# The causal mask of a decay attention, moved from matmul products into the decay rows

## What is computed

```python
c = jnp.cumsum(jax.nn.log_sigmoid(f_logit.astype(jnp.float32)), axis=1)   # per head, per token
s = jnp.einsum('bhtd,bshd->bhts', qi, k) * scale
s = s + ci[..., :, None] - c[:, :, None, :]
s = jnp.where(kpos[None, :] <= qpos[:, None], s, -jnp.inf)
p = jax.nn.softmax(s, axis=-1)
out = jnp.einsum('bhts,bshd->bthd', p, v)
```

## Time and profile before

| | |
|---|---|
| median of 3 runs | 934.23 us (931.28 to 938.12) |
| the profiled execution's own time | 933.19 us |
| its span | 931.5 us |
| TensorE busy | 912.9 us, 98% of the span |
| VectorE busy | 547.2 us, 59% |
| ScalarE busy | 301.2 us, 32% |
| the mixer's list, first scores to last | about 81 to 170 us |
| the chain that ended last | TensorE 89%, VectorE 4%, ScalarE 3% |

### The profile page before, as it was taken

One profiled execution on the slowest core, in us unless ns is written; L12 is line 12 of the kernel. 1 busy time (PEld: TensorE's weight loads), 2 busy tenths in 40 slices (PEclk: granted clock), 3 DMA queues, 4 the chain that ended last, 5 costly groups with the idle time before them and its releaser, 6 DMA issues.

```text
span 931.5 us, 13473 instructions
## 1 busy us (share of the span) xinstructions
PE 912.9 (98%) x4611; PEld 743.0 (80%) x4611; DVE 547.2 (59%) x936; ACT 301.2 (32%) x610; POOL 72.7 (8%) x138
## 2 busy tenths in 40 slices
PE   8999999999999999999999999999999999899998
PEld 7887776788888888888888888888878897568877
DVE  7257547265877677777634344686765363774554
ACT  7144466424222222222201112533321313453610
POOL 0000000010110010010001000000000000000000
PEclk9999999999999999999999999999999999999999
DMA  8756523254666556656655665476445212222554
GB/s 279 237 181 223 160 94 114 91 180 156 208 196 204 183 190 196 200 181 196 203 187 182 194 199 193 146 247 206 159 147 160 91 57 80 66 71 91 164 186 148
DMA packets 50214, 154.78 MB, mean 166 GB/s; under 512 B 9564, under 2 KB 10860, under 8 KB 50040
## 3 DMA queue, kind: packets, MB, share of 16 engines
q1 hardware_dynamic: 22320, 75.70, 25.6%
q0 software_dynamic: 19008, 69.21, 22.6%
q10 hardware_dynamic: 8840, 9.23, 3.1%
HBM read 149.63 MB, written 4.49 MB: 165 GB/s over the span
## 4 chain that ended last, share of the span: by engine, by line
PE 89%; DVE 4%; ACT 3%; issue 2%; DMA 2%; DVEq 0%; SPq 0%; POOLq 0%; ACTq 0%
PE bank L645 75%; PE bank L702 2%; DMA HI<-wstream 1%; PE bank L1054 1%; PE bank L1074 1%; PE bank L780 1%; PE bank L804 1%; PE bank L977 1%; PE bank L989 1%; PE bank L794 1%; DVE LO L1593 1%; PE bank L1004 1%; PE bank L1065 1%; DMA RAW<-wstream 0%; PE bank L783 0%
## 5 line engine op out<-in xcount | busy, mean ns | idle before, releaser
L645 PE MATMUL bank<-GH,HI 128*128 128x512 f32 (+1 forms) x724 | 292.4, 404 | 2.1 <-ACT DV L1435 1.4
L645 PE MATMUL bank<-GH,LO 128*128 128x512 f32 (+1 forms) x724 | 282.0, 390 | 0.0
L645 PE MATMUL bank<-GL,HI 128*128 128x512 f32 (+1 forms) x724 | 281.5, 389 | 0.0
L1593 DVE TENSOR_TENSOR LO<-RAW,HI 128x1024 fp32r<-128x1024 f32 x88 | 107.7, 1224 | 127.9 <-DMA HI<-wstream 127.0
L645 PEld LDWEIGHTS bank<-GH,HI 128*128 128x128 f32 x724 | 136.4, 188 | 34.9 <-issue 7.5
L645 PEld LDWEIGHTS bank<-GH,LO 128*128 128x128 f32 x724 | 136.1, 188 | 28.8
L645 PEld LDWEIGHTS bank<-GL,HI 128*128 128x128 f32 x724 | 136.6, 189 | 23.8
L627 POOL DMA_DIRECT2D HI<-wstream x132 | 70.2, 532 | 834.6 <-PE bank L645 824.7
L1309 ACT ACTIVATE YC<-AB,PAR 128x512 f32<-128x512 f32 x44 | 36.0, 819 | 140.7 <-DVE AB L1740 140.7
L645 PE MATMUL bank<-AH,HI 128*128 128x512 f32 x176 | 69.3, 394 | 0.0
L645 PE MATMUL bank<-AH,LO 128*128 128x512 f32 x176 | 69.0, 392 | 0.0
(11 more groups left out here) (304 smaller groups left out, 1209.4 us busy)
## 6 DMA issues: line engine op xcount, KB each, us to landing
RAW<-wstream SPq DMA_DIRECT2D x135, 512.0 KB, 3.7
HI<-wstream POOLq DMA_DIRECT2D x132, 512.0 KB, 4.9
X<-x_t SPq DMA_DIRECT2D x8, 256.0 KB, 7.6
NCB<-out_t ACTq DMA_DIRECT2D x4, 512.0 KB, 3.7
out_t<-X ACTq DMA_DIRECT2D x8, 256.0 KB, 5.8
XR<-out_t ACTq DMA_DIRECT2D x8, 256.0 KB, 3.6
out_t<-XR SPq DMA_DIRECT2D x7, 256.0 KB, 3.2
EG<-out_t ACTq DMA_DIRECT2D x1, 1024.0 KB, 5.1
```

Of the source, the lines that this page charges most:

```text
L645: mm = pe.matmul(out, a, b, start=(first and n == 0), stop=(last and n == 2))
L1593: dve.tensor_tensor(LO[:, u % RING, :], RAW[:, u % RING, :], HI[:, u % RING, :].bitcast(F32), ALU.subtract).then_inc(unit_split, 1)
```

## The change

The mask products, IDF, CSF and their two activations go. NCB keeps its size but is now two buffers (pairs by turns) of eight 128-element blocks for each of two heads. The DMAs of a pair (two, one per head) write the row's four blocks to places 1, 3, 5 and 7, in pieces of 512 bytes. VectorE then makes the other places in a new item `bias` p: a copy of block 0 to place 0 (2x128 elements per partition), masked copies of the blocks 0, 1, 2 at places 2, 4, 6 (2x3x128 elements, minus CAUSAL's diagonal block) and block 3 masked in place (2x128). `biased_max` reads 1 to 4 of these places with a constant stride: (2), (0, 4), (0, 3, 6) or (1, 3, 5, 7). From the third pair on, ScalarE's queue waits until the buffer's old maxima are made.

```diff
+        if n % 4 == 3 and n < 12:
+            slot.append(("bias", n // 4 + 1))
...
-    return (... + first[13:] + [("lowqk", 3)]
+    return (... + first[13:] + [("lowqk", 3), ("bias", 0)]
...
-        NCB = place("NCB", [P, 8, T], F32, arena + 80 * KB)
+        NCB = place("NCB", [P, 2, 2, 8, P], F32, arena + 80 * KB)
...
-                    pe.wait_ge(idr_made, 2)
...
-                        pe.matmul(PS[2 + e][:, 0:w], q[r, 4 + p, P * i:P * (i + 1)], k[r, p, 0:w],
-                                  start=(part == 0), stop=False)
-                for e in range(2):
-                    pe.matmul(PS[2 + e][:, P * i:w], IDF[:, :], CSF[:, :], start=False, stop=True).then_inc(s_made, 1)
+                        mm = pe.matmul(PS[2 + e][:, 0:w], q[r, 4 + p, P * i:P * (i + 1)], k[r, p, 0:w],
+                                       start=(part == 0), stop=(part == 2))
+                        if part == 2:
+                            mm.then_inc(s_made, 1)
...
-                    act.dma_start(NCB[:, 2 * n:2 * n + 2, :],
-                                  out_t[2 * n:2 * n + 2, :].unsqueeze(0).to_broadcast([P, 2, T]))\
-                       .then_inc(scratch_landed, 16)
+                    elif n >= 2:
+                        act.wait_ge(max_made, 8 * (n - 1))
+                    for e in range(2):
+                        head = out_t[2 * n + e, :].rearrange("(j c) -> j c", c=P)
+                        act.dma_start(NCB[:, n % 2, e, 1:8:2, :], head.unsqueeze(0).to_broadcast([P, NB, P]))\
+                           .then_inc(scratch_landed, 16)
...
-                dve.wait_ge(scratch_landed, 16 * (n // 4 + 1))
+                S = S.rearrange("p (j c) -> p j c", c=P)
+                bias = NCB[:, n // 4 % 2, e, (slice(2, 3), slice(0, 5, 4), slice(0, 7, 3), slice(1, 8, 2))[n % 4], :]
+                dve.wait_ge(biased, 3 * (n // 4 + 1))
...
+            def mask_bias(p):
+
+                rows = NCB[:, p % 2, :, :, :]
+                dve.wait_ge(scratch_landed, 32 * (p + 1))
+                dve.tensor_copy(rows[:, :, 0, :], rows[:, :, 1, :]).then_inc(biased, 1)
+                diagonal = CAUSAL[:, 384:512].unsqueeze(1)
+                dve.tensor_tensor(rows[:, :, 2:7:2, :], rows[:, :, 1:6:2, :],
+                                  diagonal.unsqueeze(1).to_broadcast([P, 2, 3, P]), ALU.subtract).then_inc(biased, 1)
+                dve.tensor_tensor(rows[:, :, 7, :], rows[:, :, 7, :], diagonal.to_broadcast([P, 2, P]), ALU.subtract)\
+                   .then_inc(biased, 1)
```

More of the change, by code:

```diff
@@ L61 @@
 STORED_NCB, STORED_ROWS, STORED_BETA, STORED_NT, STORED_XS = (16 * n for n in (1, 2, 3, 11, 12))
-LANDED_ROWS, LANDED_BETA, LANDED_MS, LANDED_XI = (16 * n for n in (5, 6, 7, 15))
+LANDED_ROWS, LANDED_BETA, LANDED_MS, LANDED_XI = (16 * n for n in (9, 10, 11, 19))
 _at = 0
@@ L222, in _mix1 @@
     first, last = products(0, 4), products(10, 12)
-    return (first[:3] + norms[:2] + first[3:4] + [("ncb", 0)] + _merge(first[4:13], norms[2:]) + first[13:] + [("lowqk", 3)]
+    return (first[:3] + norms[:2] + first[3:4] + [("ncb", 0)] + _merge(first[4:13], norms[2:]) + first[13:] + [("lowqk", 3), ("bias", 0)]
             + part(0, 4, products(4, 7)) + part(4, 8, _merge(products(7, 10), scaled))
@@ L379, in build @@
         SGB = place("SGB", [P, 4, P], F32, arena + 112 * KB)
-        IDF = place("IDF", [P, P], F32R, arena + 114 * KB)
-        CSF = place("CSF", [P, P], F32R, arena + 114 * KB + 512)
         assert arena + 115 * KB <= 229368, arena
@@ L506, in build @@
         sgw_masked = sem("sgw_masked")
-        idr_made, scratch_stored, scratch_landed = sem("idr_made"), sem("scratch_stored"), sem("scratch_landed")
+        biased, scratch_stored, scratch_landed = sem("biased"), sem("scratch_stored"), sem("scratch_landed")
         xs_made = sem("xs_made")
@@ L1239, in _ @@
             act.dma_start(out_t[0:8, :], FR[0:8, 2, :]).then_inc(scratch_stored, 16)
-            act.activation(IDF[:, :], IDENT, ACT.Copy).then_inc(idr_made, 1)
-            act.wait_ge(masks_landed, 16)
-            act.activation(CSF[:, :], CAUSAL[:, 384:512], ACT.Copy, scale=-1.0).then_inc(idr_made, 1)
             for what, n in MIX1_ORDER:
@@ L1652, in biased_max @@
                 S = PS[2 + e][:, 0:w]
-                dve.wait_ge(scratch_landed, 16 * (n // 4 + 1))
+                S = S.rearrange("p (j c) -> p j c", c=P)
+                bias = NCB[:, n // 4 % 2, e, (slice(2, 3), slice(0, 5, 4), slice(0, 7, 3), slice(1, 8, 2))[n % 4], :]
+                dve.wait_ge(biased, 3 * (n // 4 + 1))
                 dve.wait_ge(s_made, 2 * n + e + 1)
-                dve.tensor_tensor_reduce(S, S, NCB[:, 2 * (n // 4) + e, 0:w], -1.0, 3e38, ALU.add, ALU.min,
+                dve.tensor_tensor_reduce(S, S, bias, -1.0, 3e38, ALU.add, ALU.min,
                                          MX1[:, c:c + 1]).then_inc(max_made, 1)
+            def mask_bias(p):
[7 more added lines that the diff above has]
+                   .then_inc(biased, 1)
             for what, n in MIX1_ORDER:
@@ L1677, in _ @@
                     dve.tensor_tensor(rest, full, top.bitcast(F32), ALU.subtract).then_inc(qk_split, 1)
+                elif what == "bias":
+                    mask_bias(n)
                 elif what == "A":
```

## The result

The changed kernel takes 940.12 us (median of 20 runs, 938.17 to 944.82); the kernel before 934.14 us in 20 runs beside it. The ratio is 1.0069 with a 95% interval of 1.0056 to 1.0082: 6 us slower where 1.8 were forecast, and just past the upper end of the range (940.0). It is within 1%, so "no change by over 1%" held, but the range did not. The profiled execution took 940.21 us with a span of 938.5; that of before 933.19 and 931.5.

A forecast was written before the change was run, and what follows sets the result against it. TensorE bounds the kernel; masks about -3.0, bias0 and its stall +1.8, moved quarter +1.4, bias3, B9's wait and A11's new place +1.6 net +1.8 us: 936.0 us, range 930.5 to 940.

The forecast's parts named there:

- What bounds the kernel: TensorE, 98% busy at full clock throughout; removed work gains only where it ends last; shift at 191 us passes through.
- What the mask products cost: At the 16 mask pairs behind the scores: 0.28 us a pair by starts, 4.5 us in all.
- rival 2: Removal gives less than a pair's distance, as the following product pays the handover: 937.5 to 938.6 us; chance 0.12.
- What is added on VectorE: Each of four bias items takes 1.55 us (1.4 to 1.8); strided maxima add 0 to 0.1 us per item.
- bias0 and the first quarters: Before A1: bias0 delays A0's exponentials, A1 starts at 85.85, TensorE is +2.7 us behind after A1.
- moved quarter: One projection quarter fewer before A1, to be done afterwards: +1.4 us.
- A2 to A9: Six masks give -1.7 us, bias1 and bias2 are covered, A8's mask gives nothing; shift at A9 +1.0.
- A9 to A12: bias3 lies in full on the path before A12, which comes +1.9 to +2.4 us late; masks 11 to 14 give nothing.
- The end: A15's mask, in a full stretch, gives -0.28 us; net of the whole change +1.8 us.
- 1 (all hides): All bias items hide on VectorE: 928.3 to 929.7 us, or 932 if one partly hides; chance together 0.22.
- 3 (late rows): Row loads in 512-byte pieces take over 12 us and stall VectorE, then TensorE: 944 us or more; chance 0.03.
- 4: No work leaves TensorE's path, for instance if the new order opens an unseen wait over 2 us: 938 to 941; chance 0.06.

The follow-up runs named there:

- gap_filled: Changed kernel with 12 idle 512-column products on TensorE before A1's scores and 10 before A12's; 936.70 us, ratio 1.0034.
- early_kept: Changed kernel with the projections' quarters in their old places, bias0 behind lowqk2, last row load behind A8, bias3 behind A9; 933.86 us, ratio 1.0001.
- masks_out: Kernel before without the mask products and nothing in their place (no causal mask within the diagonal blocks); 934.16 us, ratio 0.9998.
- fills_kept: Changed kernel with the projections' quarters in the places of the kernel before, bias items put in afterwards; 937.51 us, ratio 1.0040.
- bias0_early: Changed kernel with bias0 alone moved ahead, behind lowqk2; 938.65 us, ratio 1.0054.
- order_only: Kernel before with the changed kernel's list order, bias items counted but empty, mask products kept; 935.64 us, ratio 1.0025.
- best_filled: early_kept with 3 idle products before A9's scores, 6 before A12's and 3 before A13's; 932.96 us, ratio 0.9986.

## Why the prediction was wrong, by its steps

- **What bounds the kernel**: held. TensorE is last but for the places named, and a shift at 191 us goes through to 583 us (+4.0 becomes +4.4). That the clock is full throughout was a misreading: the page's nines round away a slow stretch of 3.4 us that the kernel before has too, from 799.6 us. TensorE in order of time there:

```profile
798.30 0.52 PE L1065 MATMUL bank<-CON,P 128*128 128x128 f32 x3 [1.70 <-ACT PT L1507]
...
801.09 0.63 PE L645 MATMUL bank<-GL,HI 128*128 128x512 f32 x1
801.52 0.63 PE L645 MATMUL bank<-GH,LO 128*128 128x512 f32 x1
```

  An idle 1.70 us stands before it, so that a wait can bring the clock down could have been read before the change was run.
- **What the mask products cost**: mis-sized. 0.28 us a pair by the starts became 0.20. The products start where the mask did, as forecast, but the first one behind the scores now has 0.34 us to its successor (87.38 to 87.72 above), where behind a mask pair it had 0.28 (85.47 to 85.75), so a part of the handover stays. That is rival 2's mechanism in part, and over nine counted pairs it is +0.7 us. The formula in the Trainium skill ("VectorE: DVE Perf Modes", section on the trn2 errata) gave an estimate of 0.11 a pair. The measurement lies between the two, 0.09 above that and 0.08 below mine.
- **What is added on VectorE**: held (1.52 against 1.55), and so did the copy's and the maxima's prices.
- **bias0 and the first quarters**: the wait held to 0.1 us (A1 at 85.85 forecast, 86.49 - 0.65 = 85.84 measured). The step failed in what comes behind it: "TensorE is behind by +2.7 us after A1". I took TensorE's pace after a wait as its pace before it, since the page shows the clock full throughout. In the mixer's list it was full in a kernel whose longest wait there is 1.2 us. **The missing term is the clock: put at nothing, it cost 1.6 us between A1 and A2 in the profile, and filling both waits gives back 3.3 us of the timed runs (gap_filled)**; it is what carries the result out of the range. The sign that I gave, A1 to A8 shorter by 1.7 us, didn't come (45.84 us against 44.26), and it forgot my own moved quarter, which is done there: by my terms it should have read 0.3 shorter.
- **A2 to A9**: held, masks aside; bias1 and bias2 are covered, A8's mask gives nothing.
- **A9 to A12**: held (forecast +1.9 to +2.4 at A12; measured +4.2, of which 1.8 are the slow stretch behind A1). B9 waited 0.15 us.
- **The end**: A15's mask held with 0.2. The sum of the stalls, 1.8, stands against the 3.2 that gap_filled has left: 0.7 for the masks, 0.2 for the idle products' own length, some 0.3 for the second block in its profile.
- **Rivals**: 1 (all hides) was wrong. Even early_kept, where the items do hide, has 2.4 us of distance and not 4.5. 3 (late rows) was wrong: 6.3 us at the most. 4 named the right size for the wrong reason: no wait of over 2 us opened that I hadn't counted. None named the clock.

## What to carry to other kernels

A wait on a product engine that was always busy has two prices: its own length, and the clock behind it. Where a page shows the full clock, look with narrower windows for short slow stretches that it rounds away, and at the longest wait behind which the clock held; treat a longer one as unpriced. Work taken off TensorE in a sparse stretch lengthens the waits there, so a part of the gain can be lost to the clock (0.7 of 2.4 us in masks_out's profile); a few products whose results nobody reads may give it back. And an item that is only counted in a spread list is an edit of its own: here the moved quarters cost 1.7 us with nothing else changed.

## What the hardware did that I hadn't expected

- In the changed kernel's profile the granted clock fell to 1.2 GHz for 3.4 us, starting 1.9 us after TensorE had begun to work again behind an idle 2.88 us; not at once. In fills_kept it began 0.7 us after the start, and behind A12 it lasted 6.8 us there and in masks_out.
- The length of the wait alone doesn't tell whether it falls. In the mixer, behind an idle 1.51 us (fills_kept) and 1.54 us (masks_out) it fell; behind 1.55 us (early_kept), 1.38 us (bias0_early), 1.17 us (before) and 1.10 us (order_only) it didn't. But behind another idle 1.10 us, at a norm further on, it fell in order_only's profile:

```profile
223.42 1.05 PE L704 MATMUL bank<-CON,SQ 128*128 128x1 f32 x8 [1.10 <-DVE SQ L1577]
...
225.07 0.63 PE L647 MATMUL bank<-GH,LO 128*128 128x512 f32 x1
```

- At one place that no edit touches, around idle times of 1.1 and 1.7 us at about 800 us, the clock fell for 3.4 us in nine of the seventeen profiles, for 6.8 in six and not at all in two. From the first product with XI to the end of the span these executions take 216.6 to 217.8 us (219.2 in best_filled, with a second slow stretch at 887 us), 218.0 to 218.9 and 215.4. So nearly the same waits cost nothing in one execution and some 3 us in another, and a part of the spread of the runs is this.
- Taking out a pair of products of 128 columns, in a chain of products of 512, gave 0.20 us of the engine.
- The slowest of eight equal small DMA issues on ScalarE's queue took 1.0 to 1.7 us instead of 0.47 in eleven of the thirteen profiles of kernels without mask products, and in none of the four with them, though the edits lay 500 us earlier.
